# A two-layer hybrid decoder step: the projection's input normalised during the projection, the low-rank products in three rounded passes

## The reference

```
x += 1/2 * SwiGLU(RMSNorm(x))
h = RMSNorm(x);  proj = h @ w_in        # 6440 columns: RWKV-7, short convolution, Mamba-2
RWKV:  xs = proj + (prev_row - proj) * mu
       w = w0 + tanh(w_lr) @ w2;  a = sigmoid(a0 + a_lr @ a2);  g = sigmoid(g_lr) @ g2
       k = k * (1 + (a - 1) * k_a)      # then a recurrence over the rows
short convolution: rmsnorm(b_gate * conv3(c_gate * xt))
Mamba-2: conv4, silu, softplus(dt), a chunked scan, z gate, group norm
x += concat(three groups) @ w_out
x += 1/2 * SwiGLU(RMSNorm(x))
```

## Time and profile before

| | |
|---|---|
| median of three runs | 1659.33 us (1658.1 to 1665.26) |
| the profiled execution | 1660.52 us, its span 1658.5 us |
| TensorE busy | 1550.0 us, 93% of the span, mean granted clock 0.986 |
| VectorE, ScalarE, GpSimd busy | 1145.6, 860.9, 264.0 us |
| HBM | 242.22 MB read, 11.38 MB written, mean 155 GB/s |

### The profile page before, as it was taken

One profiled execution on the slowest core, in us unless ns is written; L12 is line 12 of the kernel. 1 busy time (PEld: TensorE's weight loads), 2 busy tenths in 40 slices (PEclk: granted clock), 3 DMA queues, 4 the chain that ended last, 5 costly groups with the idle time before them and its releaser, 6 DMA issues. The chain is left out here.

```text
span 1658.5 us, 41230 instructions
## 1 busy us (share of the span) xinstructions
PE 1550.0 (93%) x17275; PEld 1471.9 (89%) x17275; DVE 1145.6 (69%) x1832; ACT 860.9 (52%) x1521; POOL 264.0 (16%) x259
## 2 busy tenths in 40 slices
PE   7999999989799899999999999998997989899997
PEld 6999999977688789999999999998775878899997
DVE  6565578795798667665575656978768977676654
ACT  5444465767444555444354444657673445554443
POOL 0000003001455531000000000030014554300000
PEclk9999999999899999999999999999998999999999
DMA  7555557471244445555454655654703453465552
GB/s 232 178 168 176 161 157 211 131 210 52 64 127 119 138 150 171 196 174 187 149 186 153 203 166 175 194 157 131 213 1 104 126 166 111 130 199 181 187 176 71
DMA packets 280649, 256.26 MB, mean 155 GB/s; under 512 B 48054, under 2 KB 268700, under 8 KB 280450
## 3 DMA queue, kind: packets, MB, share of 16 engines
q1 hardware_dynamic: 276698, 252.05, 49.3%
q10 hardware_dynamic: 3768, 1.59, 0.4%
HBM read 242.22 MB, written 11.38 MB: 153 GB/s over the span
## 5 line engine op out<-in xcount | busy, mean ns | idle before, releaser
L209 ACT ACTIVATE front_hi<-front_raw 128x1024 fp32r<-128x1024 f32 (+2 forms) x230 | 238.5, 1039 | 257.2 <-PE ps L234 249.7
L216 DVE TENSOR_TENSOR front_lo<-front_raw,front_hi 128x1024 fp32r<-128x1024 f32 (+1 forms) x210 | 252.2, 1201 | 112.5 <-ACT front_hi L209 111.7
L209 ACT ACTIVATE out_hi<-out_raw 128x1024 fp32r<-128x1024 f32 (+1 forms) x168 | 173.2, 1038 | 216.1 <-PE ps L234 202.5
L216 DVE TENSOR_TENSOR out_lo<-out_raw,out_hi 128x1024 fp32r<-128x1024 f32 (+1 forms) x148 | 183.3, 1239 | 109.9 <-ACT out_hi L209 109.3
L232 PE MATMUL ps<-front_h_hi,front_hi 128*128 128x264 f32 (+1 forms) x816 | 241.2, 296 | 8.6 <-DVE front_lo L216 6.7
L234 PE MATMUL ps<-front_h_hi,front_lo 128*128 128x264 f32 (+1 forms) x816 | 233.0, 286 | 0.0
L233 PE MATMUL ps<-front_h_lo,front_hi 128*128 128x264 f32 (+1 forms) x816 | 232.8, 285 | 0.0
L232 PE MATMUL ps<-ffn_h_hi,out_hi 128*128 128x264 f32 x704 | 200.4, 285 | 0.1
L233 PE MATMUL ps<-ffn_h_lo,out_hi 128*128 128x264 f32 x704 | 199.6, 284 | 0.0
L234 PE MATMUL ps<-ffn_h_hi,out_lo 128*128 128x264 f32 x704 | 199.6, 283 | 0.0
L232 PE MATMUL ps<-in_h_hi,front_hi 128*128 128x264 f32 x688 | 197.3, 287 | 0.0
(11 more groups left out here) (410 smaller groups left out, 3861.2 us busy)
## 6 DMA issues: line engine op xcount, KB each, us to landing
front_raw<-in_w_in SPq DMA_DIRECT2D x50, 1024.0 KB, 5.4
out_raw<-in_ffn_w_in SPq DMA_DIRECT2D x44, 1024.0 KB, 5.2
front_raw<-in_ffn_w_in SPq DMA_DIRECT2D x40, 1024.0 KB, 5.3
back_sample_rows<-row_scratch SPq DMA_DIRECT2D x160, 128.0 KB, 3.1
out_raw<-in_w_out SPq DMA_DIRECT2D x16, 1024.0 KB, 5.8
front_raw<-in_ffn_w_out SPq DMA_DIRECT2D x16, 896.0 KB, 5.0
out_raw<-in_ffn_w_out SPq DMA_DIRECT2D x16, 896.0 KB, 4.9
front_raw<-in_ffn_w_out SPq DMA_DIRECT2D x8, 1024.0 KB, 5.4
```

Source lines behind the costliest of these rows:

```text
L209: act.activation(self.hi[n % self.RING][:, 0:k, 0:w], self._raw(n), ACT.Copy).then_inc(self.hi_ready, 1)
L216: eng.tensor_tensor(self.lo[n % self.RING][:, 0:k, 0:w], self._raw(n), self.hi[n % self.RING][:, 0:k, 0:w].bitcast(F32), ALU.subtract).the ...
```

## The change

It does three things. (1) The products of tiles 0 to 18 stay as they were, except that their input lies in the buffers of the first SwiGLU's input; for tiles from 19 on (`NORMED`) a second input, x times gain times rs, is made during slots 10 to 18: VectorE multiplies (`normed`), ScalarE rounds (`normed_hi`), VectorE subtracts (`normed_lo`), for 8 tiles through two buffers. (2) Since rs is then in the product, tiles from 19 on are evicted otherwise: `c` and `b` tiles in one multiplication on VectorE, RWKV tiles by ScalarE straight from PSUM to `xs`, after which VectorE adds the shifted rows from PSUM (`mix_shifted`). The `b` tiles move from 23 to 26 to 31 to 34, the short convolutions and the sample steps to other slots. (3) The low-rank products become three rounded passes; ScalarE makes the high parts (`lora_hi`), GpSimd the low parts (`lora_lo`), and the factor of the keys moves from ScalarE (L984) to GpSimd (`key_factor`). The logarithms and exponentials that stood ahead of `gates(5)` now stand ahead of `gates(6)`.

```diff
-                                       ("c", SC0 + 512, 0, 4), ("b", SC0, 0, 4), ("rwkv", 8 * P, 8, 8), ("rwkv", 0, 0, 8),
+                                       ("c", SC0 + 512, 0, 4), ("rwkv", 8 * P, 8, 8), ("b", SC0, 0, 4), ("rwkv", 0, 0, 8),
-        H = len(tiles)
+        H, NORMED = len(tiles), 19
-        norm2 = Norm(st, env, "mix", lambda k: env.col("norm_mix", k), A, h_hi, h_lo, rs, xa, ctmp[:, 0])
+        norm2 = Norm(st, env, "mix", lambda k: env.col("norm_mix", k), A, env.in_hi, env.in_lo, rs, xa, ctmp[:, 0])
...
+                def lora_lo(i):                              # GpSimd
+                    p0, p1, wa_hi, g_hi, stack = LORA[i]
+                    c = slice(p0 * P, p1 * P)
+                    pool.wait_ge(s("lora_hi"), 3 * i + 3)
+                    pool.tensor_tensor(wa2_lo[:, c], wa2[:, c], wa_hi[:].bitcast(F32), ALU.subtract).then_inc(s("lora_lo"), 1)
+                    pool.tensor_tensor(g2_lo[:, c], g2[:, c], g_hi[:].bitcast(F32), ALU.subtract).then_inc(s("lora_lo"), 1)
+                    pool.tensor_tensor(stack[64:96], g2b[64:96, c], stack[64:96].bitcast(F32), ALU.subtract).then_inc(s("lora_lo"), 1)
+                def key_factor(p):
+                    pool.wait_ge(s("lora_read"), 3 * p + 2)
+                    pool.tensor_scalar(mix.bonus[:, p], mix.nb[:, p], env.col("rwkv_k_a", p), env.oka[:, p:p + 1],
+                                       ALU.mult, ALU.add).then_inc(s("fac_done"), 1)
...
-                    act.wait_ge(s("lora_read"), 3 * p + 2)   # ScalarE, gates(p)
-                    act.activation(mix.bonus[:, p], mix.nb[:, p], ACT.Identity, scale=env.col("rwkv_k_a", p),
-                                   bias=env.oka[:, p:p + 1]).then_inc(s("fac_done"), 1)
+                def lora_hi(i):                              # slots 36 (i = 0), 39 (1), 42 (2)
+                    for hi, raw in ((wa_hi[:], wa2[:, c]), (g_hi[:], g2[:, c]), (stack[0:96], g2b[:, c])):
+                        act.activation(hi, raw, ACT.Copy).then_inc(s("lora_hi"), 1)
+                def normed_hi(k):                            # slots 11 (k = 0), 12 (1), 13 (2), 14 (3), 15 (4, 5), 17 (6, 7)
+                    act.wait_ge(s("normed"), k + 1)
+                    act.activation(h_hi[:, k], ctmp[:, k % 2], ACT.Copy).then_inc(s("normed_hi"), 1)
...
                     yield 13
+                    normed_hi(2)
                     act.wait_ge(s("btok_ps"), 1)
                     act.activation(btok[:].rearrange("p c g n -> p (c g n)"), ps[:, A, :], ACT.Copy).then_inc(s("btok_done"), 1)
...
                     more.go(n)
+                    if kind == "rwkv" and n >= NORMED:
+                        act.wait_ge(ws.used, base + n + 1)
+                        bank = ps[:, n % 3, 0:N]
+                        act.activation(mix.xs[:, m], bank, ACT.Copy, scale=env.omu[:, m:m + 1]).then_inc(kept, 1)
+                        act.activation(last[:, m], bank[:, T - 1:T + NS], ACT.Copy).then_inc(last_in, 1)
                     ws.split_hi(act, base + n + 4)
...
+                    if kind == "c":                          # VectorE, evict
+                        dve.wait_ge(evicted, n)
+                        dve.tensor_tensor(u[:, m, 2:2 + N], u[:, m, 2:2 + N], bank, ALU.mult).then_inc(evicted, 1)
+                        return
+                    if kind == "b":
+                        dve.wait_ge(s("smp_sc"), 5)
+                        dve.wait_ge(s("uconv"), 3 * (m + 1))
+                        dve.tensor_tensor(acc[:, m], acc[:, m], bank, ALU.mult).then_inc(evicted, 1)
+                        return
+                def mix_shifted(n, m):
+                    dve.wait_ge(kept, q + 1)
+                    dve.wait_ge(last_in, q + 1)
+                    dve.scalar_tensor_tensor(out=mix.xs[:, m, 1:T], in0=bank[:, 0:T - 1], scalar=env.col("rwkv_mu", m),
+                                             in1=mix.xs[:, m, 1:T], op0=ALU.mult, op1=ALU.add).then_inc(evicted, 1)
+                def normed(k):                               # slots 10 (k = 0), 11 (1), 12 (2), 13 (3), 14 (4, 5), 16 (6, 7)
+                    if k >= 2:
+                        dve.wait_ge(s("normed_lo"), k - 1)
+                    dve.scalar_tensor_tensor(out=ctmp[:, k % 2], in0=env.x[:, k], scalar=env.col("norm_mix", k), in1=rs[:],
+                                             op0=ALU.mult, op1=ALU.mult).then_inc(s("normed"), 1)
+                def normed_lo(k):                            # slots 12 (k = 0), 13 (1), 14 (2, 3), 16 (4, 5), 18 (6, 7)
+                    dve.wait_ge(s("normed_hi"), k + 1)
+                    dve.tensor_tensor(h_lo[:, k], ctmp[:, k % 2], h_hi[:, k].bitcast(F32), ALU.subtract).then_inc(s("normed_lo"), 1)
...
+                def lora(p):                                 # TensorE
+                    for n, (w, x) in enumerate(((wa_hi[:, own], lr_hi), (wa_hi[:, own], lr_lo), (wa2_lo[:, c], lr_hi))):
+                        for h, bank in enumerate((A, DB)):
+                            mm = pe.matmul(ps[:, bank, 0:N], w[half[h]], x[half[h], 0:N], start=n == 0, stop=n == 2)
+                    pe.matmul(gate, g_hi[:, own], lr_hi[:, N:2 * N], start=True, stop=False)
+                    pe.matmul(gate, g_hi[:, own], lr_lo[:, N:2 * N], start=False, stop=False)
+                    pe.matmul(gate, g2_lo[:, c], lr_hi[:, N:2 * N], start=False, stop=False)
+                    pe.matmul(gate, stack[0:96, own], lr_stack[:], start=False, stop=True).then_inc(s("lora_ps"), 1)
```

224 lines of the change are left out of this document (153 added, 71 removed).

## The result

The changed kernel takes 1711.04 us (median of 4 runs, 1706.68 to 1719.79) against 1661.48 for the kernel before (4 runs): a ratio of 1.030, 95% interval 1.026 to 1.035, slower. I had forecast slower, but by 25 us where it is 50: 1684 with a range of 1657 to 1700, so the time lies outside it. The profiled execution took 1712.41 (span 1710.6).

The account below looks back on a forecast made before the run. TensorE, busy 93% of the span, was taken as the bound, with VectorE the bound in slots 27 to 38. Per layer 16.0 + 2.5 - 6.0 = +12.5, +25 for both, gave 1684 us, range 1657 to 1700.

Parts of the forecast that it names:

- Slots 10 to 19: Where the normalisation is added: new VectorE and ScalarE work delays TensorE's L1443, +16.0 us per layer, bounds +6.1 and +17.6.
- the clock: Slots 10 to 19: TensorE's idle times lower the granted clock to 0.97, a loss of 1.6 us, used only in the upper bound.
- The walk: Slots 10 to 19, instruction by instruction: L1443 of slot 13 starts 6.6 us late, slot 15 10.4, slot 17 13.7, slot 19 16.0.
- the sentence on the bounds: Slots 10 to 19: +6.1 us without the lock, +17.6 with TensorE idle 3 to 5 us at a time and clock 0.97.
- Slots 25 to 38: +2.5 us per layer: VectorE, the bound there, gets relief, but late RWKV tiles wait for ScalarE; bounds -7.9 and +5.
- the relief of 5.1 us on VectorE: Slots 25 to 38: eleven fewer evictions to `prev` (-3.9) and one product with `b_gate` less (-1.2).
- The delay at tile 26: Slots 25 to 38: ScalarE copies tile 26 only behind decays, so VectorE's first sample addition comes 2.4 us later.
- Slots 39 to 50: -6.0 us per layer: cheaper low-rank products -8.6, new waits for gates(0) +2.0 and gates(6) +3.9, shorter r_k and kk_norm waits -3.3.
- the seven passes: Slots 39 to 50: ten rounded matmuls per low-rank product, six in pairs, make seven passes of 0.12, 0.85 us.
- The lock does not stack: Rival, slots 10 to 19: GpSimd's low parts fall beside PSUM-reading instructions; 2.6 us per layer, 1664.5 us, chance 0.20.
- Faster: Rival: VectorE's list decides slots 25 to 38, TensorE's 7.9 us idle goes; -7.8 per layer, 1644 us, chance 0.16.
- ScalarE binds too: Rival, from slot 25 on: none of the 2.5 gained, low-rank pairs don't pair, clock falls; 1698 us, chance 0.09.

Follow-up runs that it names:

- warm: The changed kernel with 36, 33 and 25 unused matmuls on TensorE at slots 13, 15 and 17, filling its waits: 1703.9 us, ratio 1.028.
- behind_spread: The changed kernel with normalisation work queued behind what TensorE waits for, plus ScalarE's sample-state decays spread over slots 25, 26, 28 and 31: 1673.0 us, ratio 1.010.
- no_normed: The changed kernel without the eight normed, normed_hi and normed_lo per layer, products from tile 19 on reading constants: 1665.0 us, ratio 1.004.
- dve_lows: The changed kernel with the low parts of weights 16, 18, 20 and 22 on VectorE instead of GpSimd: 1685.7 us, ratio 1.016.

## Why the prediction was too low

**Slots 10 to 19: +16.0, measured +23.7 and 21.7** (6.7 + 17.0 in layer 0; 5.9 + 15.8 in layer 1). The step that failed is one term of this sum, the clock: priced at 1.6 us as the end of a range and left out of the 16.0, it measured 7.0 in layer 0. The walk itself held. `b_tok` queued behind three `normed_hi`, the holds of 2.1 us and the order ahead of `segments` are all in the trace, at the place and with the size that I had: slot 13 at 272.84 (272.8 forecast), the hold of `normed(2)` at 269.39, the waits of 4.5, 4.1 and 3.2. (At slot 19, where I had also written 3 to 5, TensorE waits 0.8, after 0.9 inside product 19.) What I left out stood in the sentence on the bounds: idle times of 3 to 5 us and a granted clock of 0.97 elsewhere, "a loss of 1.6 us". I read the loss as the mean of a stretch in which TensorE's longest wait was 2.5 us (for `outer`), and not of 3 to 5, and its idle time 7.9 of 55. The price of one such wait stood in the same trace, in the rows behind it, and I did not look:

```profile
337.38 1.16 PE L1405 MATMUL ps<-bc_rows,pick_row 16*128 16x256 f32 x8 [2.47 <-DVE outer L1173]
339.27 0.42 PE L234 MATMUL ps<-front_h_hi,front_lo 128*128 128x264 f32 x1
```

That product took 4.4 us instead of 2.9. Three times that loss of 1.5 would have put 4.6 us per layer into the sum. Measured, the three products cost 2.3 each, 7.0 us, and 16.0 + 7.0 = 23.0; in layer 1, where the first costs 1.5, 6.2 and 22.2. *warm* shows the term by itself. The rule that the default is the low level and that activity releases it stands in the Trainium skill, "TensorE: Matmul & The Clock Gate", Part 1; the runs agree: the granted clock is 0.50 behind the three waits, and 1.00 when useless matmuls fill them.

**Slots 25 to 38: +2.5, measured +7.5.** TensorE's idle time grew by 2.3 us, what my sum of waits had; the other 5.2 are half clock, the same missing term. The 2.3 is in part luck, since the waits are not the ones I had: the relief of 5.1 us on VectorE was on the wrong engine, and ScalarE bound from slot 25 to 28 (*behind_spread*, -5). The delay at tile 26 (2.4) is there; the one at tile 25, with `xdt` and L1626 behind it, was missing (3.0). About 1.4 of the 7.5 comes with the normalisation (*no_normed*): the product behind slot 19 takes 4.4 instead of 2.9.

**Slots 39 to 50: -6.0, measured -1.4 and -4.1.** The three-pass product takes 1.16, not 0.85: it is the seven passes that I had, six matmuls in three pairs and four single ones, but the first of each of the two groups takes 0.22 instead of 0.12, and so does the change from one group to the other. So 8 x 0.77 = 6.2 instead of 8.6. The 2.0 more for `gates(0)` did not come (0.26 and 0.53, before 0.49 and 0.20). The wait for `gates(6)` is 2.9 (3.9 forecast). The waits for `r_k` and `kk_norm` shrank by 0.1 and 0.7, not 3.3: the last one is 3.24 instead of 3.01; I take it for the end of a chain of gates, scan and `r_k` that starts with TensorE's last product. The two layers differ by 2.7 us, and their waits are nearly the same: it is the clock. Both wait 2.9 us for `gates(6)`, but the product behind takes 4.6 us in layer 0 (granted clock 0.57, first row) and 2.8 in layer 1 (1.00, second row):

```profile
448.90:453.50 4.60, 4.60 (x25) 4.60 (x25) 2.44 (x3) 2.60 (x6) 3.02 (x4) 0.57 0.00 0
1291.20:1294.10 2.90, 2.90 (x27) 2.90 (x26) 2.79 (x4) 2.87 (x8) 1.61 (x1) 1.00 0.00 0
```

**The rivals.** *The lock does not stack* fell: the holds are in the rows, four per layer. *Faster* fell: `mix_shifted(26)` waits 2.6 us and L1443 of slot 13 waited for `b_tok` until 272.84, both beyond the points that I had named. *ScalarE binds too* was right in its place, and its 1698 was the nearest number, but its pairs did pair, and it too had only 1.6 us per layer for the clock.

The sum of the parts as measured is 29.7 and 25.0 us for the two layers; the span grew by 52.1, so the rest of the program gave 2.6 back. Of the 17.2 us that layer 0 lies above my 12.5, 7.0 are half clock in the first stretch and 5.2 in the second; 4.6 come from the last one, where the products, the clock and the waits each have a part.

## What to carry to other kernels

Where a change makes the fullest engine wait for microseconds, charge the wait and then the next product at half clock, and carry that delay into the next turn of the cycle. Look in the trace on hand for a wait of that size and read the rows behind it. It is an estimate for the worst case: a wait of 2.9 us was followed by a slow product in one layer and by none in the other. A background job costs what it delays, not what it takes: put behind the instructions that are waited for, the same 24 instructions cost 4.4 us in slots 10 to 19 of layer 0 instead of 23.7, and about 7 per layer in all. When an eviction moves to another engine, list that engine's long blocks (decays, logarithms with their table loads) first: each of them now holds the accumulation banks.

## What the runs showed that I had not expected

A matmul of 264 columns takes 0.42 instead of 0.28 us for one product after waits of 3.2 to 4.5 us, and after the waits of 1.6 and twice 0.24 inside tile 19 too; after 2.0 to 2.5 us in *dve_lows* the product took 4.4 instead of 5.2, and after 2.9 us in layer 1 of the changed kernel it took the full-clock 2.8. Fourteen matmuls in a wait of 1.6 us brought 2.8 us.

The hold between VectorE and GpSimd goes both ways: GpSimd's low part of 32 rows took 0.99 in some kernels and layers and 1.88 in others, and through the instruction behind it, and the clock behind that, goes with 3 to 6 us per layer (62.6 against 69 in the last stretch). Each kernel has one profile, so whether the same engine comes first in every execution of a kernel is not shown, and a single profile of that stretch should not be trusted.
